# Expert rows read in halves: gathered first halves, second halves read densely for two tiles at a time

## What is computed

```python
def _peer(h, p):                      # h: 1152 x 1024
    qh = (ht @ p['pk_w_q']).reshape(t, 8, 2, 128)
    s = jnp.einsum('thpd,phkd->pthk', qh, p['pk_sub_keys'])      # 8 heads, 2 x 128 keys
    sv, si = lax.top_k(s, 16)
    cand = (sv[0][..., :, None] + sv[1][..., None, :]).reshape(t, 8, 256)
    cidx = (si[0][..., :, None] * 128 + si[1][..., None, :]).reshape(t, 8, 256)
    best, pos = lax.top_k(cand, 16)
    eidx = jnp.take_along_axis(cidx, pos, axis=-1)               # 128 experts a token
    gate = jax.nn.softmax(best, axis=-1)
    act = jax.nn.gelu(jnp.einsum('td,thkd->thk', hb, u_tab[eb]))
    return jnp.einsum('thk,thkd->td', gb * act, v_tab[eb])       # u_tab, v_tab: 16384 x 1024
```

## Time and profile before

| | us |
|---|---|
| median of three runs | 3967.75 |
| lowest, highest | 3966.49, 3968.9 |
| span of the profiled execution | 3962.1 |
| first dot product of tile 0 | 881.74 |
| first dot product of tile 2 (group 128) | 1604.51 |
| last result stored from | 3959.02 |

### The profile page before, as it was taken

The page is one execution under the profiler, slowest core; times in us unless marked ns, Lnnn a source line. Parts: engine busy times, 40 slices in busy tenths (PEclk is TensorE's granted clock), DMA queues, the critical chain, the costliest instruction groups (busy, mean ns, idle before and its releaser), DMA issues.

```text
span 3962.1 us, 46323 instructions
## 1 busy us (share of the span) xinstructions
PE 2943.4 (74%) x16906; PEld 1316.2 (33%) x16906; DVE 2784.1 (70%) x6805; ACT 676.6 (17%) x1388; POOL 1319.1 (33%) x1174
## 2 busy tenths in 40 slices
PE   8999999979899997856666666656656666665555
PEld 3666665545444442213222222212212222221111
DVE  4545647746787786756888868877877786887555
ACT  2534533011121221000111110111101111101000
POOL 0000000014444443333444444444544444444443
PEclk9999999989899998988878878878877878886777
DMA  4010004459999999999999999999999999999998
GB/s 184 23 35 26 23 25 157 170 207 410 413 415 414 408 403 415 418 423 413 414 396 413 418 416 409 416 410 420 415 411 414 418 414 408 415 416 407 418 421 343
DMA packets 214904, 1346.40 MB, mean 340 GB/s; under 512 B 24818, under 2 KB 45810, under 8 KB 63762
## 3 DMA queue, kind: packets, MB, share of 16 engines
q0 software_dynamic: 165888, 1208.03, 74.2%
q1 hardware_dynamic: 47636, 133.32, 9.0%
q10 hardware_dynamic: 1152, 2.10, 0.1%
HBM read 1329.69 MB, written 13.67 MB: 339 GB/s over the span
## 4 chain that ended last, share of the span: by engine, by line
DMA 37%; PE 35%; DVE 13%; issue 11%; POOL 2%; ACT 1%; POOLq 0%; SPq 0%; DVEq 0%; ACTq 0%
DMA arena<-in_uv,mask_b 14%; PE ps L782 12%; DMA arena<-in_uv,mask_f 12%; DMA arena<-in_uv,ones 11%; PE ps L1453 9%; DVE arena L1294 4%; PE ps L760 3%; PE ps L647 3%; POOL arena L616 2%; DVE arena L1176 2%; PE ps L1447 2%; PE ps L711 1%; PE ps L678 1%; DVE arena L1136 1%; PE ps L1505 1%
## 5 line engine op out<-in xcount | busy, mean ns | idle before, releaser
L782 PE MATMUL ps<-arena 64*64 64x512 f32 x9216 | 1461.6, 761 | 943.0 <-DVE arena L1176 929.3
L1294 DVE CUSTOM_DVE_ANT_0 arena<-arena 128x1024 f32<-128x1024 f32 x1152 | 1411.7, 1226 | 738.3 <-DMA arena<-in_uv,mask_b 285.1
L782 PEld LDWEIGHTS ps<-arena 64*64 64x64 f32 x9216 | 351.4, 158 | 1896.4 <-DVE arena L1176 1380.3
L616 POOL DMA_INDIRECT arena<-in_uv,ones x384 | 448.3, 1167 | 635.0 <-PE ps L782 467.4
L616 POOL DMA_INDIRECT arena<-in_uv,mask_f x384 | 441.8, 1150 | 586.7 <-PE ps L782 493.4
L616 POOL DMA_INDIRECT arena<-in_uv,mask_b x384 | 423.2, 1102 | 601.9 <-PE ps L782 514.6
L973 ACT ACTIVATE arena<-arena 128x2 f32<-128x2 f32 x576 | 117.3, 204 | 2641.0 <-DVE arena L1294 2565.6
L1453 PE MATMUL ps<-arena 128*128 128x384 f32 x1152 | 384.1, 489 | 1.8 <-DVE arena L1740 1.8
L1176 DVE TENSOR_SCALAR arena<-arena 128x64 f32<-128x64 f32 x1152 | 308.0, 310 | 0.3 <-ACT arena L973 0.3
L760 PE MATMUL ps<-arena 128*128 128x384 f32 x768 | 268.6, 497 | 0.0
L598 POOL IOTA arena<- 128x16 f32 x1 | 0.1, 145 | 793.3 <-PE ps L660 793.3
(11 more groups left out here) (203 smaller groups left out, 2360.7 us busy)
## 6 DMA issues: line engine op xcount, KB each, us to landing
arena<-in_w_mg SPq DMA_DIRECT2D x16, 1536.0 KB, 21.2
arena<-in_w_in SPq DMA_DIRECT2D x28, 512.0 KB, 3.3
arena<-in_w_mod SPq DMA_DIRECT2D x8, 1792.0 KB
arena<-in_w_mod SPq DMA_DIRECT2D x4, 2048.0 KB, 23.3
arena<-in_w_out SPq DMA_DIRECT2D x2, 4096.0 KB, 16.8
arena<-in_w_q SPq DMA_DIRECT2D x8, 1024.0 KB, 14.2
arena<-in_w_q SPq DMA_DIRECT2D x4, 2048.0 KB
arena<-x_scratch SPq DMA_DIRECT2D x15, 512.0 KB, 11.2
```

What stands on the lines that cost most here:

```text
L616: nc.gpsimd.indirect_dma_start(out=RG[n % RING], out_offset=None, in_=uv, in_offset=bass.IndirectOffsetOnAxis(ap=EIDX[t % 3][:, s:s + 1], ...
L782: mm = nc.tensor.matmul(PS[c * HALF:(c + 1) * HALF, 2 * r + n, :], DG[rows, s, :], RG[s][rows, D + n * 512:D + (n + 1) * 512], start=(g == ...
L1294: ins = v.tensor_tensor_reduce(u, u, h2, 1.0, 0.0, ALU.mult, ALU.add, PRE[:, s % RING:s % RING + 1])
```

## The change

Tiles 0 and 1 (NA = 2) stay as they are. For tiles 2 to 8 the table is seen as 32768 half rows (`u_rows`), the key numbers are doubled, and GpSimd gathers only the u half of each row, 4 KB, into a ring `UB` of six buffers. A buffer is free when VectorE's dot product has read it (`dots`). The results of a whole tile are collected in `DOTS`; one GELU a tile (`tile_gelu`) and one product with the gates (`coefs`) make the coefficients.

The v halves are not gathered. The tiles form teams, (2, 3), (4, 5), (6, 7) and (8). After the last dot product of a team, a dense matrix `COEF` is built, for each first key number i1 (128), each second key number (the partition) and each token of the team. For this TensorE turns the two key numbers and the coefficients of a tile (`turn`), so that a token is a column. A block is four tokens. For each, a one-hot matrix of the second key numbers (`full_hots`, on ScalarE, as Relu(1 - |x|)) is multiplied on TensorE (`block`) with a one-hot matrix of the first ones (`key_hots`, on VectorE, by comparison), whose rows ScalarE has scaled with the coefficients (`scale_part`). ScalarE copies the result to `COEF` (`block_out`). Two blocks stand in a group's place. There are 64 blocks for a team of two and 32 for the last.

Then SyncE reads the whole v half of the table in 128 chunks of 128 rows of 4 KB, four buffers `VB` deep, and TensorE multiplies each with its slice of `COEF`, two products of 128x512 for each tile of the team (`values`). VectorE reads the sums at `ends_at`, 112 groups' places after the build's start. With 64 groups a tile the builds begin at groups 258, 386, 514 and 638, the ends at 370, 498, 626 and 750; dot products end with group 575.

The mixes, norms and transposes of the late tiles now all stand in groups 117 to 157, their rows go through DRAM, and their queries are made together (`late_query`, 256 products of 384 columns). All late scores go through DRAM, and ScalarE issues the reads back. The experts of tiles 3 and 4 are looked for from groups 170 and 214 on.

```diff
+NA = 2
+TEAMS = ((2, 3), (4, 5), (6, 7), (8,))
...
+UR = 6
+VR = 4
...
-MIX_AT, MIX_STEP = 117, 3
+MIX_AT, MIX_GAP = 117, 6
+LATE_QUERIES_AT, LATE_QUERIES_GAP = 158, 11
...
+    C_W = 2 * P
+    COEF = AR[:, 0:P * C_W].rearrange("p (i t) -> p i t", t=C_W)
+    hi = lambda n: AR[:, P * C_W + n * D:P * C_W + (n + 1) * D]
+    VB = [hi(0), hi(1), AR[:, A_END - 2 * D:A_END - D], AR[:, A_END - D:A_END]]
...
+    u_rows = uv.rearrange("e (h d) -> (e h) d", h=2)
...
+    def build_at(g):
+        done = (TEAMS[g][-1] + 1) * GROUPS + 2
+        return max(done, ends_at(g - 1) + 12) if g else done
...
+    def ends_at(g):
+        return build_at(g) + 112
...
+        def chunk(g, i1):
+            n = g * P + i1
+            if n >= VR:
+                sp.wait_ge(v_done, n - VR + 1)
+            sp.dma_start(VB[n % VR], uv[i1 * P:(i1 + 1) * P, D:2 * D]).then_inc(l_v[n % VR], 16)
...
-                    out=RG[n % RING], out_offset=None, in_=uv,
-                    in_offset=bass.IndirectOffsetOnAxis(ap=EIDX[t % 3][:, s:s + 1], axis=0),
-                ).then_inc(gathered[n % RING], 16)
+                m = n - NA * SLOTS
+                if t < NA:
+                    nc.gpsimd.indirect_dma_start(
+                        out=RG[n % RING], out_offset=None, in_=uv,
+                        in_offset=bass.IndirectOffsetOnAxis(ap=EIDX[t % 3][:, s:s + 1], axis=0),
+                    ).then_inc(gathered[n % RING], 16)
+                else:
+                    if m < UR:
+                        wait_alone(pool, v_used, n + 1 - RING)
+                    else:
+                        wait_alone(pool, dots, (n - UR) // GRP + 1)
+                    nc.gpsimd.indirect_dma_start(
+                        out=UB[m % UR], out_offset=None, in_=u_rows,
+                        in_offset=bass.IndirectOffsetOnAxis(ap=EIDX[t % 3][:, s:s + 1], axis=0),
+                    ).then_inc(u_in[m % UR], 16)
...
+            for z, x in enumerate((*KEYNO[(t - NA) % 4], DOTS[t % 2])):
+                mm = nc.tensor.transpose(PS[:, 4 + 2 * j, z * P:(z + 1) * P], x, ident[:])
+            mm.then_inc(tu_r, 1)
...
+        def block(g, n):
+            b_, k = n % 2, blocks_before[g] + n
+            pe.wait_ge(part_r, k + 1)
+            pe.wait_ge(full_r, FULLS + 2 * k + 2)
+            if k >= 2:
+                pe.wait_ge(c_r, k - 1)
+            for u in range(4):
+                mm = nc.tensor.matmul(PS[:, 5 + 2 * b_, u * P:(u + 1) * P], FULL[b_][:, u], PART[b_][:, u],
+                                      start=True, stop=True)
+            mm.then_inc(built, 1)
...
+            for i1 in range(P):
+                n = g * P + i1
+                pe.wait_ge(l_v[n % VR], V_LOADS + 16 * (n // VR + 1))
+                for j in range(len(TEAMS[g])):
+                    for half in range(2):
+                        mm = nc.tensor.matmul(PS[:, 2 * j + half, :], COEF[:, i1, j * P:(j + 1) * P],
+                                              VB[n % VR][:, half * 512:(half + 1) * 512],
+                                              start=(i1 == 0), stop=(i1 == P - 1))
+                mm.then_inc(v_done, 1)
...
+            b.at(build_at(g) + 1 + len(team) * P // 8, lambda g=g: values(g))
...
+        def tile_gelu(t):
+            act.wait_ge(dots, (t + 1) * GROUPS)
+            A(DOTS[t % 2], DOTS[t % 2], ACT.Gelu_apprx_tanh).then_inc(dots_gel, 1)
...
+        def full_hots(g, n):
+            b_, k = n % 2, blocks_before[g] + n
+            j, q = divmod(n, P // 4)
+            if k == 0:
+                act.wait_ge(st_sc[1], 16 * (PAIRS * (TILES - 1) // 2))
+            elif k >= 2:
+                act.wait_ge(built, k - 1)
+            for u in range(4):
+                ins = A(FULL[b_][:, u], iota2, ACT.Abs, scale=-1.0, bias=TURNED[j][:, 1, 4 * q + u:4 * q + u + 1])
+            ins.then_inc(full_r, 1)
+            act.wait_ge(full_r, FULLS + 2 * k + 1)
+            A(FULL[b_], FULL[b_], ACT.Relu, scale=-1.0, bias=1.0).then_inc(full_r, 1)
...
+        def scale_part(g, n):
+            b_, k = n % 2, blocks_before[g] + n
+            j, q = divmod(n, P // 4)
+            act.wait_ge(oh_r, k + 1)
+            for u in range(4):
+                ins = A(PART[b_][:, u], PART[b_][:, u], ACT.Copy, scale=TURNED[j][:, 2, 4 * q + u:4 * q + u + 1])
+            ins.then_inc(part_r, 1)
...
+            act.wait_ge(built, k + 1)
...
+            A(COEF[:, :, j * P + 4 * q:j * P + 4 * q + 4], PS[:, 5 + 2 * b_, :].rearrange("p (u i) -> p i u", u=4),
+              ACT.Copy).then_inc(c_r, 1)
...
+                    dve.wait_ge(v_done, (self.g + 1) * P)
+                    sums = PS[:, 2 * self.j:2 * self.j + 2, :].rearrange("p b c -> p (b c)")
+                    v.tensor_tensor(self.y, sums, G2B, ALU.mult).then_inc(acc_read, 1)
...
+        def coefs(t):
+            dve.wait_ge(dots_gel, GELUS + t - NA + 1)
+            v.tensor_tensor(DOTS[t % 2], DOTS[t % 2], GATE[t % 3], ALU.mult).then_inc(coef_r, 1)
...
+            elif k >= 2:
+                dve.wait_ge(built, k - 1)
+            shape = [P, 4, P]
+            v.tensor_tensor(PART[b_], iota2.unsqueeze(1).to_broadcast(shape),
+                            TURNED[j][:, 0, 4 * q:4 * q + 4].unsqueeze(2).to_broadcast(shape),
+                            ALU.is_equal).then_inc(oh_r, 1)
...
+                    dve.wait_ge(u_in[m % UR], U_LOADS + 16 * (m // UR + 1))
+                    if s % SLOTS == 0 and t >= NA + 2:
+                        dve.wait_ge(tu_r, t - NA - 1)
+                    u, to = UB[m % UR], DOTS[t % 2][:, s % SLOTS:s % SLOTS + 1]
```

More of the change, by code:

```diff
@@ L59 @@
 PIECE = 2 * P
+NA = 2
+TEAMS = ((2, 3), (4, 5), (6, 7), (8,))
+assert [t for team in TEAMS for t in team] == list(range(NA, TILES)) and NA < EARLY
+UR = 6
+VR = 4
+LATE_PART = (T - TA) // 2
 P_LB, P_CW, P_CB, P_BR, P_BI, P_LAM, P_HN, P_H0, NPAR = 0, 4, 8, 9, 11, 13, 15, 16, 18
@@ L427, in run, with run_rest @@
                 step()
+        def run_rest(self):
+            for group in sorted(self.steps):
+                self.run(group)
     def stage_b_sp(sp, ends_out):
@@ new lines, in rows_in @@
+        def rows_in(t):
+            sp.dma_start(rows_of(t), h2_d[t]).then_inc(l_h2[t % 3], 16)
+        sp.wait_ge(mix_r, TILES)
+        query_weights(0)
+        query_weights(1)
+        sp.wait_ge(h2_st, 16)
+        for t in range(TILES - 2, TILES):
+            sp.wait_ge(h2_late[t % 2], h2_stores(t))
+        sp.wait_ge(dots, 2 * GROUPS)
+        sp.wait_ge(v_used, NA * SLOTS)
+        for t in range(NA + 1, NA + 4):
+            rows_in(t)
+        for i in (2, 3):
+            sp.wait_ge(lq_r, (i - 1) * 8)
+            query_weights(i)
@@ new lines, in stage_b_sp @@
+        sp.dma_start(G2C, row(mod_d[0, 5 * D:6 * D])).then_inc(l_end, 16)
+        end_rows()
+        for t in range(NA):
+            end_in(t, t)
+            sp.dma_start(EY[t], sum_d[t]).then_inc(l_end, 16)
+        def chunk(g, i1):
[3 more added lines that the diff above has]
+            sp.dma_start(VB[n % VR], uv[i1 * P:(i1 + 1) * P, D:2 * D]).then_inc(l_v[n % VR], 16)
+        for i1 in range(VR):
+            chunk(0, i1)
+        for t in range(NA):
+            finished(t, t)
@@ new lines, in stage_b_sp @@
+        for g, team in enumerate(TEAMS):
+            for i1 in range(VR, P):
+                chunk(g, i1)
+                if i1 == ENDS_FREE + VR:
+                    for j, t in enumerate(team):
+                        end_in(t, j)
+                    end_rows()
+            if g + 1 < len(TEAMS):
+                if team[-1] + 3 < TILES:
+                    sp.wait_ge(dots, (team[0] + 3) * GROUPS)
+                    rows_in(team[0] + 4)
+                for i1 in range(VR):
+                    chunk(g + 1, i1)
+            for j, t in enumerate(team):
+                finished(t, j)
+            if team[-1] + 4 < TILES:
+                sp.wait_ge(dots, (team[0] + 4) * GROUPS)
+                rows_in(team[0] + 5)
@@ L829, in stage_b_pe @@
+        for g, team in enumerate(TEAMS):
+            for t in team:
+                b.at(build_at(g), lambda t=t: turn(t))
+            for n in range(len(team) * P // 4):
+                b.at(build_at(g) + 1 + n // 2, lambda g=g, n=n: block(g, n))
+            b.at(build_at(g) + 1 + len(team) * P // 8, lambda g=g: values(g))
+        for t in range(NA):
             for g in range(GROUPS):
@@ L975, in stage_b_act @@
             after.run(n)
-        turned_sums(TILES - 1)
-        end(TILES - 1)
+        b.run(NA * GROUPS)
+        after.run_rest()
+        b.run_rest()
     def stage_b_dve(dve):
@@ L1298, in stage_b_dve @@
             b.run(n)
-        coef(TILES * GROUPS - 1)
-        end = End(TILES - 1)
-        for step in (end.read_sums, end.add_sums, end.scale, end.residual, end.square, end.norm):
-            step()
+        b.run_rest()
     block = ctx.enter_context(nc.Block())
```

528 lines of the change are left out of this document (321 added, 207 removed), and 3 rows, old and new, of the table EARLY_TOP_AT.

## The result

| | us |
|---|---|
| kernel before, median of four runs | 3968.32 (3966.49 to 3969.77) |
| changed kernel, median of four runs | 4744.84 (4742.19 to 4751.26) |
| ratio | 1.196 [1.194, 1.198] |
| forecast | 4387, range 4180 to 4600 |

A forecast was written before the change was run, and what follows sets the result against it. DMA was taken to bound the kernel; with that limit gone, phases follow one another: 1604.5 + 515 + 3 x 253 + 2 x 385 + 2 x 55 + 290 + 16 + 130 + 175 + 12 = 4381.5, plus 5.7: 4387 us, range 4180 to 4600.

The forecast's parts named there:

- What bounds the kernel, and what goes: DMA at 413 GB/s bounds tiles 2 to 8; 201 MB less traffic gives at most 487 us.
- the price of a chunk: Passes over the second halves: four TensorE products of 474 ns, 1.9 us a chunk, 243 us a pass for two tiles.
- the 363 us of traffic: First two passes: 150 MB of chunks and gathers at 413 GB/s end last; 385 us taken for each pass.
- the third pass: Tiles 6 and 7: 29 groups of dots left, about 122 us, then 88 chunks at 1.9 us: 290 us.
- the last pass: Tile 8 alone: 67.1 MB at 413 GB/s, set by DMA above TensorE's 122 us; 175 us, ends 163 and 200.
- the builds: Making COEF: ScalarE bounds at 3.9 us a block (3.5 to 4.5), VectorE waits; 253 us three times, then 130.
- stage A: Groups 128 to 257, up to the first build: 515 us, ends 485 and 560, late queries costed at nothing.
- the ends: After each of the first two passes, 16 groups and two tile ends, 55 us; after the third, 16 us.
- The first: Rival: unknown prices at upper ends, blocks 4.5 us, shared passes 413, final pass 200: 4602 us; chance 0.12.
- The second: Rival: ScalarE doesn't bound block building, which goes at VectorE's pace, 483 us instead of 889: 3981 us; chance 0.06.
- third: Rival: as The second, and gathers and chunks share DMA without a gap, 363 twice instead of 385: 3937 us; chance 0.05.
- the fourth: Rival: gathers of 4 KB rows take as long as 8 KB rows, about 5.1 us a group: about 4900 us; chance 0.04.

The follow-up runs named there:

- the experiment: Changed kernel with only a quarter of the late queries' products done (two of eight steps of the sum over the width): 4691.84 us, ratio 1.183.
- the version with little else: Changed kernel with two blocks a tile instead of 32 and 32 chunks a pass instead of 128, multiplied with the identity; gathers and dot products whole: 3548.41 us, ratio 0.894.

## Why the prediction was wrong in size

**What bounds the kernel, and what goes: right.** 1604.5 against 1615 for the first dot product of tile 2, q0 at 738 MB, and the DMA limit gone outside the passes.

**The failed step is the price of a chunk**: "A chunk of 0.52 MB feeds four products of 128x512, 474 ns each (64.0 us for 135): 1.9 us, 243 a pass". 474 ns is the price of a record, and a product has two. With 3.5 us a chunk the same reasoning gives 448 a pass for two tiles and 224 for one, against 451, 450, 450, 245 measured. TensorE would then have stood above the 363 us of traffic in the first two passes, and the third pass, which has no full second half of gathers, would have been no shorter than the others. This one term is 66 + 65 + 160 = 291 us, and most of the last pass's 70. The count stood in the row; I divided busy time by it and did not hold it against the loop. The two experiments on the pass show it from both sides: half the products give 305 us in all, nearly all chunk bytes away 40. With this price mended the passes of the sum come to 3 x 448 + 224 = 1568 instead of 1235, and the forecast to 4720 against 4745. That it would be so near is in part luck: the builds, 103 us too high, cancel stage A and the ends, 105 too low with the changeover.

**The last pass** (175 against 245) had a second fault behind the first: with TensorE's price mended it would be 224, and reads at four in flight give 291 GB/s, not the 413 of the earlier trace rows, which the gathers of whole rows reach and these reads only with ten in flight (410). It costs some 25 us here (245 against the 220 with ten buffers), and 64 where TensorE has half the work (229 against 165). The Trainium skill, DMA: Bandwidth & Descriptors (Bandwidth), gave an estimated 197 for this pass by its 341 GB/s; the runs show less with four reads in flight and more with ten.

**Stage A** (515 against 602) failed at "I cost them at nothing": the late queries' 512 records fill TensorE for 215 us. The bound of 45 us that the text gave for it had the size nearly right, against 55 in the experiment, for another wait: it is not the fourth pair of tile 3 that waits for the queries but the first (23.5 us), and then the exponentials of the first two (21.0 and 10.2).

**The builds: mechanism right, size 103 us too high**, some 10 of it by the place of the turnings as said. A block took 3.48 us, just under the lower end of 3.5 to 4.5. Four activations with a pointer take 1.26 us on the timeline, 386 to 389 ns each with an overlap of some 95 ns:

```profile
2300.89 0.63 ACT L1158 ACTIVATE arena<-arena 128x512 f32<-128x512 f32 x1
...
2301.42 1.26 ACT L1166 ACTIVATE arena<-arena 128x128 f32<-128x128 f32 x4
...
2302.59 0.57 ACT L1181 ACTIVATE arena<-ps 128x512 f32<-128x512 f32 x1
```

I had drawn "no overlap" from three 384-column activations that carry other waits. The Trainium skill, ScalarE: Activation LUTs (What ACT_TABLE_LOAD costs), gave an estimated 3.6 us a block by its formula, and the trace agrees to 0.1 us: the page was nearer than my reading of the row. The Trainium skill's rule (ScalarE: Activation LUTs, Rules for kernel authors) that multiply and relu belong on VectorE held for the relu: moving that one-hot there was worth 203 us. The scaling stayed on ScalarE in every run, so for the multiply no run here shows it. VectorE's wait for blocks, forecast as 3 x 100 us, was 320. ScalarE's busy time rose by 610, not by 800. Some 716 us follow on the start of the last dot product (4028 to 4744), not 500.

**Rivals.** The first had the right sign of the error. Its largest term went the other way, since blocks were cheaper and not dearer; the passes were dearer as it had them, but by TensorE's price and not by their share of DMA. The second and third fall with ScalarE busy 220 of 225 us in a build (the 38 us that the second had for the last build hold the same slip, four products of 0.29 us that are eight records), the fourth with 3.9 us a group for half rows. The range of 4180 to 4600 left the time out, since no bound was drawn around the price of a product, which I took for known. Two small sums of the prediction do not come out, and nothing hangs on them: VectorE's work alone in stage A makes 491 (515 less 40 groups x 0.6), not 485, and the upper end of a pass 272 + 76 x 1.9 = 416, not 413.

## What to carry to other kernels

Before a row's busy time is divided by its count, hold the count against the loop in the code: if the row has twice as many, one operation is two instructions, and every price from that row doubles. Where a limit that hides everything is taken away, price each phase on each engine again, the ones that had been far below the limit too, and add the phases that stand in a row: here builds on ScalarE and passes on TensorE alternate, so neither is ever hidden by the other. A gain in bytes (201 MB, at most 487 us) is worth only as much as the new chain allows; here the kernel became 777 us longer.

## What the runs showed of the hardware

- A float32 product of 128x512 takes 0.88 us at a clock of 0.99 and shows as two instructions whose recorded durations (599 ns) overlap. A product's price is read from starts, not from the mean duration.
- The granted clock followed the work: 0.50 (1.2 GHz) in the first build, where TensorE is busy 133 of 225 us in short bursts; 0.99 (2.4 GHz) in the pass. In the builds that did no harm, since ScalarE set the pace.
- Reads of 0.52 MB with next to nothing beside them: 291 GB/s with four in flight, 385 with ten over the whole pass and 410 in its middle. The median to landing went from 5.9 to 11.6 us.
- In the version with little else DMA moved 318 GB/s between 2600 and 3000 us; an estimate from the 202 gathers of 0.52 MB in that stretch is 265 for the gathers of 4 KB rows alone. VectorE was busy 335 of the 400 us, so this is no limit of the gathers. Those of 8 KB rows ran at 413.
